# Feed-forwards: one 512-column and one 256-column matmul in place of three of 256, with the second half added by VectorE

## The chip, the cores and the metric

One core of a Trainium2 chip runs the whole program. The metric is the device time of one execution in microseconds (us).

## What is computed

Ten layers run one after the other on a sequence of 256 tokens of width 1024, in float32: an attention layer, feed-forward, convolution, feed-forward, neighbourhood attention, feed-forward, retention, feed-forward, convolution, feed-forward. Each is x + layer(norm(x)). The feed-forward (five of them) is

```python
h = _rmsnorm(x, norm_ffn_pre[l])
u = _dwconv(h @ w_up[l], conv_w[l], conv_b[l])
g, v = u[..., :D_FF], u[..., D_FF:]
y = (jax.nn.gelu(g, approximate=True) * v) @ w_down[l]
```

with D_FF = 2816 and a depthwise convolution of three taps along the tokens. The four later ones are of the same form.

## The kernel before

Tokens lie along the free axis (S = 256 columns) for the up products, and features on the 128 partitions. Every float32 factor is split in two parts, high (rounded to the format of the fast matmul) and low (the rest), and a product is three matmuls: high x high, low weight x high activation, high weight x low activation (`product`, lines 1971 to 1973; for the down products lines 2069 to 2071, with the activations as the stationary operand and 512 weight columns streamed). A matmul is always preceded by the load of its stationary operand.

All weights come as a stream of chunks of 128 x 2048 through a ring of three slots. SyncE loads chunk c into `raw` once the low part of chunk c - 3 is made; ScalarE makes the high part (`split_hi`, line 668; in the feed-forward loop `loop_split`, line 889) once TensorE is through with chunk c - 3; VectorE then makes the low part (`split_lo`, line 1154, and `loop_split`, line 1474); TensorE waits for that low part (`lo_done`) before it uses the chunk. Instructions of one engine run in the order in which they are written.

A feed-forward (`ffn`, on TensorE line 2156, ScalarE line 865, VectorE line 1424) has 22 tiles of 128 features. An up chunk holds the weights of one tile for both halves g and v: 2 x 8 steps of three 256-column matmuls, 48 in all. A down chunk serves two tiles: 24 matmuls of 512 columns into four banks. TensorE's order of chunks is up 0, 1, 2, 3, down 0, then up 4, 5, down 1 and so on to up 20, 21, down 9, and down 10. Chunk numbers in the text are those of this order; chunk 3 is the fourth up chunk and chunk 4 the first down chunk.

What happens to a tile behind its up chunk: VectorE scales both halves by the tokens' reciprocal roots (`up_norm`, line 1433); ScalarE makes the centre tap and bias (`centre`, line 877, two instructions); VectorE adds the outer taps (`taps`, line 1447, four instructions); ScalarE the gelu of half g (line 882); VectorE the product of the halves (`gated_value`, line 1456), its high part by a copy (`parts`, line 1466) and its low part (line 1468). The down chunk waits for that low part (`ulo_done`). The row of roots reaches every partition by a matmul in the second up chunk (`root_row`, line 1967), is copied by ScalarE (line 800), and VectorE's `up_norm(0)` waits for it.

The order on VectorE in a pair of tiles i is: parts(2i-2), low split of the second up chunk of the pair, low split of the down chunk, up_norm(2i), gated_value(2i-1), parts(2i-1), taps(2i), up_norm(2i+1), low split of the next pair's first up chunk, gated_value(2i), taps(2i+1).

In the neighbourhood attention (`attention`, lines 813 and 1346) ScalarE makes the high parts of the output projection's chunks 13 and 14 in four halves (`half_hi_of`, line 677) between the exponentials of the heads, and GpSimd their low parts in four pieces of 512 each (`low_parts`, line 587).

## Time and profile before

| | |
|---|---|
| time, median of 3 runs | 1617.42 us (1616.62 to 1617.46) |
| the profiled execution | 1617.76 us, span 1616.0 us |
| TensorE busy | 1594.0 us, 99% |
| VectorE busy | 1212.8 us, 75% |
| ScalarE busy | 897.1 us, 56% |
| GpSimd busy | 97.7 us, 6% |
| weights and other data read | 282.43 MB |

The time and the span are of the same execution; the 1.8 us between them lie outside the first and the last instruction. Busy times are of instructions; matmuls are pipelined and overlap in the record, so a mean duration of one is longer than what it holds TensorE up. The granted clock is a share of TensorE's full speed of 2.4 GHz.

### The profile page before, as it was taken

To read this page: it belongs to the slowest core of one execution; us is meant where nothing else is said; L and a number is where in the kernel's file an instruction comes from. 1 tells how busy PE (TensorE), PEld (TensorE's weight loads), DVE (VectorE), ACT (ScalarE), POOL (GpSimd) and SP (SyncE) were. 2 spreads that over 40 slices of the span, in tenths; PEclk is the share of its full clock that TensorE was granted. 3 is DMA by queue.
4 is the path that set the end of the run, shared out by engine and by line. 5 is a ranking of instruction groups with operands and counts; after the bars stand their busy time and mean duration, and the time that the engine had idled before them with its cause. 6 is when DMAs were issued, how large, how long until landed. Compare 5 with 4: busy or idle time off the path is not lost.

```text
span 1616.0 us, 28651 instructions
## 1 busy us (share of the span) xinstructions
PE 1594.0 (99%) x10570; PEld 1443.0 (89%) x10570; DVE 1212.8 (75%) x1828; ACT 897.1 (56%) x1190; POOL 97.7 (6%) x102
## 2 busy tenths in 40 slices
PE   9999999999999999989999999999999999999999
PEld 9888999978899999869999998878999987899998
DVE  6757887778787877856877886456787887878787
ACT  6576554565655546665544554544645456664553
POOL 0031000000000001330000042000100000000000
PEclk9999999999999999999999999999999999999999
DMA  9435545443654453443555455534554544345453
GB/s 344 147 115 178 199 182 204 160 169 118 241 187 178 182 208 133 171 142 131 184 190 198 180 185 183 203 109 157 175 214 169 184 179 183 133 155 204 185 182 130
DMA packets 43394, 285.48 MB, mean 177 GB/s; under 512 B 5280, under 2 KB 5408, under 8 KB 10688
## 3 DMA queue, kind: packets, MB, share of 16 engines
q1 hardware_dynamic: 40592, 274.96, 46.6%
q0 software_dynamic: 2736, 9.60, 1.8%
q8 instruction: 46, 0.75, 0.2%
q14 instruction: 20, 0.16, 0.0%
HBM read 282.43 MB, written 1.05 MB: 175 GB/s over the span
## 4 chain that ended last, share of the span: by engine, by line
PE 90%; DVE 5%; ACT 2%; issue 2%; DMA 1%; SPq 0%; POOL 0%; DVEq 0%; ACTq 0%
PE bank L1971 16%; PE bank L1973 16%; PE bank L1972 16%; PE bank L2069 8%; PE bank L2070 8%; PE bank L2071 8%; PE bank L2019 4%; PE bank L2020 4%; PE bank L2021 4%; PE bank L1953 1%; PE bank L2468 1%; DVE w_lo L1154 1%; PE bank L2130 1%; DMA x<-x_in 1%; DVE w_lo L1474 0%
## 5 line engine op out<-in xcount | busy, mean ns | idle before, releaser
L1971 PE MATMUL bank<-h_hi,w_hi 128*128 128x256 f32 x2220 | 633.5, 285 | 4.0 <-issue 2.3
L1972 PE MATMUL bank<-h_hi,w_lo 128*128 128x256 f32 x2220 | 630.2, 284 | 0.0
L1973 PE MATMUL bank<-h_lo,w_hi 128*128 128x256 f32 x2220 | 630.2, 284 | 0.0
L1971 PEld LDWEIGHTS bank<-h_hi,w_hi 128*128 128x128 f32 x2220 | 425.7, 192 | 11.2 <-issue 6.9
L1972 PEld LDWEIGHTS bank<-h_hi,w_lo 128*128 128x128 f32 x2220 | 425.7, 192 | 3.0
L1973 PEld LDWEIGHTS bank<-h_lo,w_hi 128*128 128x128 f32 x2220 | 425.6, 192 | 0.8
L1474 DVE TENSOR_TENSOR w_lo<-raw,w_hi 128x2048 fp32r<-128x2048 f32 x145 | 327.5, 2284 | 3.9 <-ACT w_hi L889 3.9
L877 ACT ACTIVATE arena<-arena,par 128x256 f32<-128x256 f32 x220 | 120.3, 594 | 352.2 <-DVE arena L1433 348.9
L1154 DVE TENSOR_TENSOR w_lo<-raw,w_hi 128x2048 fp32r<-128x2048 f32 (+3 forms) x108 | 232.8, 2156 | 103.3 <-ACT w_hi L668 103.2
L889 ACT ACTIVATE w_hi<-raw 128x2048 fp32r<-128x2048 f32 x150 | 286.2, 1908 | 19.8 <-PE bank L2071 19.8
L2069 PE MATMUL bank<-w_hi,h_hi 128*128 128x512 f32 x632 | 248.2, 393 | 1.5 <-DVE h_lo L1468 1.5
L2070 PE MATMUL bank<-w_lo,h_hi 128*128 128x512 f32 x632 | 246.6, 390 | 0.0
L2071 PE MATMUL bank<-w_hi,h_lo 128*128 128x512 f32 x632 | 246.0, 389 | 0.0
L668 ACT ACTIVATE w_hi<-raw 128x2048 fp32r<-128x2048 f32 (+3 forms) x105 | 187.9, 1791 | 102.0 <-PE bank L2071 38.9
L1447 DVE SCALAR_TENSOR_TENSOR arena<-arena,par 128x255 f32<-128x255 f32 x440 | 183.2, 478 | 22.4 <-ACT arena L877 22.4
L1433 DVE TENSOR_TENSOR arena<-bank,rs_row 128x512 f32<-128x512 f32 x110 | 76.0, 690 | 117.3 <-PE bank L1973 110.4
L2069 PEld LDWEIGHTS bank<-w_hi,h_hi 128*128 128x128 f32 x632 | 118.9, 188 | 27.1 <-issue 3.7
L2071 PEld LDWEIGHTS bank<-w_hi,h_lo 128*128 128x128 f32 x632 | 118.7, 188 | 25.2
L2070 PEld LDWEIGHTS bank<-w_lo,h_hi 128*128 128x128 f32 x632 | 118.9, 188 | 22.5 <-issue 0.2
L2019 PE MATMUL bank<-w_hi,h_hi 128*128 128x512 f32 x308 | 120.8, 392 | 0.1
L2020 PE MATMUL bank<-w_lo,h_hi 128*128 128x512 f32 x308 | 119.9, 389 | 0.0
L2021 PE MATMUL bank<-w_hi,h_lo 128*128 128x512 f32 x308 | 119.9, 389 | 0.0
(229 smaller groups left out, 1323.6 us busy)
## 6 DMA issues: line engine op xcount, KB each, us to landing
raw<-wstream SPq DMA_DIRECT2D x252, 1024.0 KB, 4.8
raw<-wstream SPq DMA_DIRECT2D x8, 256.0 KB, 3.8
raw<-wstream SPq DMA_DIRECT2D x4, 512.0 KB, 7.5
arena<-dilated_bias POOLq DMA_DIRECT2D x8, 256.0 KB, 4.7
arena<-conv_rows POOLq DMA_DIRECT2D x2, 1024.0 KB, 4.9
arena<-window_bias POOLq DMA_DIRECT2D x4, 512.0 KB, 5.8
raw<-wstream SPq DMA_DIRECT2D x4, 384.0 KB, 3.4
cst<-consts SPq DMA_DIRECT2D x1, 1088.0 KB, 12.6
```

The source lines that it names most:

```text
L668: nc.scalar.activation(w_hi[:, c % RING, 0:w], raw[:, c % RING, 0:w], ACT.Copy).then_inc(hi_done, 1)
L889: nc.scalar.activation(w_hi[:, c % RING, :], raw[:, c % RING, :], ACT.Copy).then_inc(hi_done, 1)
L1154: nc.vector.tensor_tensor(w_lo[:, s, 0:w], raw[:, s, 0:w], w_hi[:, s, 0:w].bitcast(F32), ALU.subtract)\
L1474: nc.vector.tensor_tensor(w_lo[:, c % RING, :], raw[:, c % RING, :], w_hi[:, c % RING, :].bitcast(F32), ALU.subtract).then_inc(lo_done, 1)
L1971: nc.tensor.matmul(dst, w_parts[0], x_parts[0], start=start, stop=False, **kw)
L1972: nc.tensor.matmul(dst, w_parts[1], x_parts[0], start=False, stop=False, **kw)
L1973: return nc.tensor.matmul(dst, w_parts[0], x_parts[1], start=False, stop=stop, **kw)
L2019: nc.tensor.matmul(dst, a, w[0], start=not second and t == 0, stop=False, skip_group_check=True)
L2020: nc.tensor.matmul(dst, a, w[1], start=False, stop=False, skip_group_check=True)
L2069: nc.tensor.matmul(dst, hi, w[0], start=first and a == 0, stop=False, skip_group_check=True)
L2070: nc.tensor.matmul(dst, hi, w[1], start=False, stop=False, skip_group_check=True)
L2071: last = nc.tensor.matmul(dst, lo, w[0], start=False, stop=last_ and a == 1, skip_group_check=True)
```

## The change

The high and the low part of the activations move into one array, side by side (`h_both`), and the eight banks of the accumulator become one array, two neighbouring banks for each of the two tiles in flight (`up_banks`). An up step is one matmul of 512 columns (high weights over high and low activations, into the two halves of a bank) and one of 256 (low weights over high activations, into the first half). ScalarE then copies the second halves of both banks to SBUF (`low_sums`), VectorE adds the first halves (`up_sum`) and in a second instruction scales. The high part of the gated product moves from VectorE to ScalarE (`high_part`), and the orders on both engines change; an up chunk waits for the add of the tile two before it, from tile 2 on. Row sums of the feed-forwards go to another bank. In the neighbourhood attention GpSimd makes both parts of chunks 13 and 14 (`both_parts`). Elsewhere views follow the new layout, with the same counts and widths. The diff, cut to what the text speaks of:

```diff
-        h_hi = sb("h_hi", [P, 16, S], F32R)
-        h_lo = sb("h_lo", [P, 16, S], F32R)
+        h_both = sb("h_both", [P, 16, 2, S], F32R)
+        h_hi, h_lo = h_both[:, :, 0, :], h_both[:, :, 1, :]
...
-        bank = [ctx.enter_context(nc.psum_tensor(f"bank{i}", [P, 512], F32)) for i in range(8)]
+        psum = ctx.enter_context(nc.psum_tensor("bank", [P, 8, 512], F32))
+        bank = [psum[:, (i + 1) % 8, :] for i in range(8)]
...
+        def up_banks(a):
+            return psum[:, 2 * a:2 * a + 2, :]
+        def row_bank(name):
+            return bank[DOWN0] if name.startswith("ffn") else stat
...
+        up_l = region(2560, 2, 512)
...
+            def both_parts(c, piece):
+                pool.wait_ge(raw_full[c % RING], 16 * (c // RING + 1))
+                pool.wait_ge(chunk_used, c - RING + 1)
+                pool.wait_ge(hi_done, c)
+                pool.wait_ge(lo_done, c)
+                for at in range(0, widths[c], piece):
+                    part, end = slice(at, at + piece), at + piece == widths[c]
+                    nc.gpsimd.tensor_copy(w_hi[:, c % RING, part], raw[:, c % RING, part]).then_inc(hi_done if end else piece_hi, 1)
+                    k["piece"] += not end
+                    pool.wait_ge(*((hi_done, c + 1) if end else (piece_hi, k["piece"])))
+                    last = nc.gpsimd.tensor_tensor(w_lo[:, c % RING, part], raw[:, c % RING, part],
+                                                   w_hi[:, c % RING, part].bitcast(F32), ALU.subtract)
+                last.then_inc(lo_done, 1)
...
-                        low_parts(c0 + c, 512)
+                        both_parts(c0 + c, 512)
...
+                def low_sums(t, a, used):
+                    act.wait_ge(chunk_used, used)
+                    if not isinstance(t, int) or t >= 2:
+                        act.wait_ge(up_sum, t + (T0 - 1))
+                    nc.scalar.activation(halves(up_l[:, a, :]), up_banks(a)[:, :, S:2 * S], ACT.Copy).then_inc(up_low, 1)
+                def high_part(t, slot, used=None):
+                    act.wait_ge(prod_done, t + (T0 + 1))
+                    if used is not None:
+                        act.wait_ge(chunk_used, used)
+                    nc.scalar.activation(h_hi[:, slot, :], u32[:, slot % 2, :], ACT.Copy).then_inc(uhi_done, 1)
+                low_sums(0, 0, c0 + 1)
                 centre(0, 0)
+                low_sums(1, 1, c0 + 2)
                 split_hi(c0 + 3)
                 centre(1, 1)
                 gelu(0, 0)
                 gelu(1, 1)
                 with act.Fori(1, FT // 2) as i:
+                    high_part(i * 2 + (-2), 8, i * 3 + (c0 - 1))
                     loop_split(i, 0)
-                    for a in range(2):
-                        centre(i * 2 + a, a)
-                        loop_split(i, 1 + a)
-                        gelu(i * 2 + a, a)
+                    high_part(i * 2 + (-1), 9, i * 3 + (c0 - 1))
+                    low_sums(i * 2, 0, i * 3 + c0)
+                    centre(i * 2, 0)
+                    loop_split(i, 1)
+                    low_sums(i * 2 + 1, 1, i * 3 + (c0 + 1))
+                    gelu(i * 2, 0)
+                    centre(i * 2 + 1, 1)
+                    loop_split(i, 2)
+                    gelu(i * 2 + 1, 1)
+                high_part(FT - 2, 10)
+                high_part(FT - 1, 11)
...
-                    attention((0, 1, 2), None, {2: lambda: half_hi_of(c0 + 13, 0), 3: lambda: half_hi_of(c0 + 13, 1),
-                                                5: lambda: half_hi_of(c0 + 14, 0), 6: lambda: half_hi_of(c0 + 14, 1)},
+                    attention((0, 1, 2), None, {},
...
+                    act.wait_ge(hi_done, c0 + 15)
...
-                def up_norm(t, a, bank_, used):
-                    dve.wait_ge(chunk_used, used)
+                def up_norm(t, a):
+                    dve.wait_ge(up_low, t + (T0 + 1))
                     if not isinstance(t, int) or t >= 2:
                         dve.wait_ge(taps_done, t * 4 + (4 * T0 - 4))
-                    nc.vector.tensor_tensor(halves(up_n[:, a, :]), halves(bank[bank_][:, :]),
+                    nc.vector.tensor_tensor(halves(up_n[:, a, :]), up_banks(a)[:, :, 0:S], halves(up_l[:, a, :]), ALU.add)\
+                             .then_inc(up_sum, 1)
+                    dve.wait_ge(up_sum, t + (T0 + 1))
+                    nc.vector.tensor_tensor(halves(up_n[:, a, :]), halves(up_n[:, a, :]),
                                             rs_row[:, :].unsqueeze(1).broadcast_to([P, 2, S]), ALU.mult).then_inc(up_ready, 1)
...
-                def parts(t, a, d_used=None):
-                    dve.wait_ge(prod_done, t + (T0 + 1))
-                    slot = 8 + a
-                    if d_used is None:
-                        slot = 10 + a
-                    else:
-                        dve.wait_ge(chunk_used, d_used)
-                    nc.vector.tensor_copy(h_hi[:, slot, :], u32[:, a, :]).then_inc(uhi_done, 1)
+                def low_part(t, slot):
                     dve.wait_ge(uhi_done, t + (T0 + 1))
-                    nc.vector.tensor_tensor(h_lo[:, slot, :], u32[:, a, :], h_hi[:, slot, :].bitcast(F32), ALU.subtract)\
+                    nc.vector.tensor_tensor(h_lo[:, slot, :], u32[:, slot % 2, :], h_hi[:, slot, :].bitcast(F32), ALU.subtract)\
                              .then_inc(ulo_done, 1)
...
                 prenorm(gain, c0)
-                up_norm(0, 0, c0 % 3, c0 + 1)
-                up_norm(1, 1, (c0 + 1) % 3, c0 + 2)
+                up_norm(0, 0)
+                up_norm(1, 1)
                 taps(0, 0)
                 split_lo(c0 + 3)
                 taps(1, 1)
                 gated_value(0, 0)
                 def two_tiles(i):
 
-                    used = i * 3 + (c0 - 1)
-                    parts(i * 2 + (-2), 0, used)
                     if not isinstance(i, int):
                         loop_split(i, -1)
+                    gated_value(i * 2 + (-1), 1)
+                    low_part(i * 2 + (-2), 8)
+                    low_part(i * 2 + (-1), 9)
+                    up_norm(i * 2, 0)
                     loop_split(i, 0)
-                    up_norm(i * 2, 0, (c0 + 2) % 3, i * 3 + c0)
-                    gated_value(i * 2 + (-1), 1)
-                    parts(i * 2 + (-1), 1, used)
                     taps(i * 2, 0)
-                    up_norm(i * 2 + 1, 1, (c0 + 3) % 3, i * 3 + (c0 + 1))
+                    up_norm(i * 2 + 1, 1)
                     loop_split(i, 1)
                     gated_value(i * 2, 0)
                     taps(i * 2 + 1, 1)
@@ -1500,9 +1551,9 @@
                 two_tiles(1)
                 with dve.Fori(2, FT // 2) as i:
                     two_tiles(i)
-                parts(FT - 2, 0)
                 gated_value(FT - 1, 1)
-                parts(FT - 1, 1)
+                low_part(FT - 2, 10)
+                low_part(FT - 1, 11)
...
-                def up(t, c, slot_c, between=None):
+                def up(t, a, c, slot_c, wait_h=None, between=None):
 
                     pe.wait_ge(lo_done, c + 1)
-                    if not isinstance(t, int) or t >= 3:
-                        pe.wait_ge(up_ready, t + (T0 - 1))
-                    for m in range(2):
-                        for kt in range(8):
-                            last = product(bank[slot_c % 3][:, m * S:(m + 1) * S], weights(slot_c, (8 * m + kt) * P),
-                                           h_parts(kt), kt == 0, kt == 7)
-                            if between and (m, kt) == (1, 2):
-                                between()
+                    if not isinstance(t, int) or t >= 2:
+                        pe.wait_ge(up_sum, t + (T0 - 1))
+                    steps = [(m, kt) for m in range(2) for kt in range(8)]
+                    if wait_h is not None:
+                        steps = [(m, kt) for kt in range(8) for m in range(2)]
+                    for m, kt in steps:
+                        if wait_h is not None and m == 0:
+                            pe.wait_ge(hlo_done, wait_h + kt + 1)
+                        w, dst = weights(slot_c, (8 * m + kt) * P), up_banks(a)[:, m, :]
+                        nc.tensor.matmul(halves(dst), w[0], h_both[:, kt, :, :], start=kt == 0, stop=kt == 7, skip_group_check=True)
+                        last = nc.tensor.matmul(dst[:, 0:S], w[1], h_hi[:, kt, :], start=False, stop=kt == 7, skip_group_check=True)
+                        if between and (m, kt) == (1, 2):
+                            between()
                     last.then_inc(chunk_used, 1)
...
-                feature_chunk(c0, wait_h=k["hlo"])
-                up(1, c0 + 1, c0 + 1, root_row)
-                up(2, c0 + 2, c0 + 2)
-                up(3, c0 + 3, c0 + 3)
+                up(0, 0, c0, c0, wait_h=k["hlo"])
+                up(1, 1, c0 + 1, c0 + 1, between=lambda: root_row(bank[DOWN0]))
+                up(2, 0, c0 + 2, c0 + 2)
+                up(3, 1, c0 + 3, c0 + 3)
                 down(0, c0 + 4, c0 + 4, first=True)
                 with pe.Fori(2, FT // 2) as i:
                     for a in range(2):
-                        up(i * 2 + a, i * 3 + (c0 - 1 + a), c0 + 2 + a)
+                        up(i * 2 + a, a, i * 3 + (c0 - 1 + a), c0 + 2 + a)
                     down(i - 1, i * 3 + (c0 + 1), c0 + 4)
```

## Rows read from the trace of the kernel before

**Rows 1.** Page, part 1: busy time, share of the span and instructions of each engine
```profile
PE 1594.0 (99%) x10570; PEld 1443.0 (89%) x10570; DVE 1212.8 (75%) x1828; ACT 897.1 (56%) x1190; POOL 97.7 (6%) x102
```

**Rows 2.** Groups by shape, TensorE: busy us, mean ns of one, idle before
```profile
L1971 PE MATMUL bank<-h_hi,w_hi 128*128 128x256 f32 x2200 | 625.6, 284 | 4.0 <-issue 2.3 <-DVE w_lo L1154 0.6 <-DVE w_lo L1277 0.3
```

**Rows 3.** Timeline, TensorE, second feed-forward (start us, us, engine, line)
```profile
430.62 0.35 PE L1971 MATMUL bank<-h_hi,w_hi 128*128 128x256 f32 x1
...
440.40 0.60 PE L1967 MATMUL bank<-hn,cst 128*128 128x256 f32 x2
...
440.95 0.28 PE L1972 MATMUL bank<-h_hi,w_lo 128*128 128x256 f32 x1
...
454.02 0.28 PE L1973 MATMUL bank<-h_lo,w_hi 128*128 128x256 f32 x1
...
454.14 0.40 PE L2069 MATMUL bank<-w_hi,h_hi 128*128 128x512 f32 x1
...
459.38 0.39 PE L2071 MATMUL bank<-w_hi,h_lo 128*128 128x512 f32 x1
...
459.82 0.38 PE L1971 MATMUL bank<-h_hi,w_hi 128*128 128x256 f32 x1
```

**Rows 4.** Timeline, VectorE, head of the second feed-forward
```profile
441.45 0.69 DVE L1433 TENSOR_TENSOR arena<-bank,rs_row 128x512 f32<-128x512 f32 x1 [1.32 <-ACT rs_row L800]
...
443.43 1.66 DVE L1447 SCALAR_TENSOR_TENSOR arena<-arena,par 128x255 f32<-128x255 f32 x4
...
445.11 2.29 DVE L1154 TENSOR_TENSOR w_lo<-raw,w_hi 128x2048 fp32r<-128x2048 f32 x1
...
449.68 0.43 DVE L1468 TENSOR_TENSOR h_lo<-arena,h_hi 128x256 fp32r<-128x256 f32 x1
...
450.88 2.29 DVE L1474 TENSOR_TENSOR w_lo<-raw,w_hi 128x2048 fp32r<-128x2048 f32 x1 [0.77 <-ACT w_hi L889]
```

**Rows 5.** Timeline, ScalarE, the same head
```profile
441.03 0.39 ACT L800 ACTIVATE rs_row<-bank 128x256 f32<-128x256 f32 x1 [1.71 <-PE bank L1967]
...
442.18 1.09 ACT L877 ACTIVATE arena<-arena,par 128x256 f32<-128x256 f32 x2 [0.76 <-DVE arena L1433]
...
443.18 1.90 ACT L668 ACTIVATE w_hi<-raw 128x2048 fp32r<-128x2048 f32 x1
...
447.37 0.42 ACT L882 ACTIVATE arena<-arena 128x256 f32<-128x256 f32 x1
```

**Rows 6.** Groups by shape, ScalarE and VectorE: nearest shapes to the added work
```profile
L998 ACT ACTIVATE h_hi<-arena 128x256 fp32r<-128x256 f32 x16 | 6.4, 420 | 6.5 <-DVE arena L1651 6.5
...
L988 ACT ACTIVATE arena<-bank 128x512 f32<-128x512 f32 x12 | 6.3, 599 | 4.4 <-PE bank L2268 4.4
...
L1896 DVE TENSOR_TENSOR arena<-arena 128x512 f32<-128x512 f32 x8 | 5.4, 689 | 1.9 <-ACT arena L1113 1.9
```

**Rows 7.** Timelines, TensorE and VectorE, tail of the second feed-forward
```profile
607.26 0.40 PE L2069 MATMUL bank<-w_hi,h_hi 128*128 128x512 f32 x1
...
607.57 0.69 DVE L1433 TENSOR_TENSOR arena<-bank,rs_row 128x512 f32<-128x512 f32 x1 [1.82 <-PE bank L1973]
...
612.62 0.42 DVE L1468 TENSOR_TENSOR h_lo<-arena,h_hi 128x256 fp32r<-128x256 f32 x1
...
613.19 0.47 PE L2069 MATMUL bank<-w_hi,h_hi 128*128 128x512 f32 x1 [0.30 <-DVE h_lo L1468]
```

**Rows 8.** Neighbourhood attention: timelines, stretches with granted clock, GpSimd's group
```profile
698.95 1.04 ACT L677 ACTIVATE w_hi<-raw 128x1024 fp32r<-128x1024 f32 x1
...
706.87 0.64 PE L2382 MATMUL bank<-cst,arena 128*128 128x128 f32 x2 [0.98 <-ACT arena L827]
...
703.55:706.96 3.41, 2.05 (x37) 1.34 (x36) 2.49 (x10) 3.41 (x8) 3.29 (x3) 1.00 0.01 2
...
706.97:710.38 3.41, 3.41 (x32) 2.52 (x32) 1.39 (x4) 2.21 (x8) 3.40 (x3) 0.50 0.65 226
...
L587 POOL TENSOR_TENSOR w_lo<-raw,w_hi 128x512 fp32r<-128x512 f32 x20 | 24.8, 1272 | 10.7 <-ACT w_hi L677 10.5
```

47 lines of the change are left out of this document (25 added, 22 removed).

## Prediction, made before the changed kernel ran

> **What bounds the kernel now.** The page comes first: TensorE is busy for 99% of the span and VectorE for 75% [rows 1], so a change that shortens TensorE's stream shortens the kernel, as long as the engines that feed it stay ahead. Then the groups by shape: the product helper (lines 1971 to 1973) issues 2200 steps of three 256-column matmuls [rows 2]; 22 tiles x 16 steps x 5 feed-forwards = 1760 of them are the ones that change. The mean of 284 ns is no price, since matmuls overlap; the price is the distance from start to start. In the second feed-forward 110 of the 256-column matmuls start between 440.95 and 454.02: 13.07 us over 109 distances, 120 ns; 24 of the 512-column ones start from 454.14 to 459.38: 5.24 us over 23, 228 ns [rows 3]. A matmul thus costs about 12 to 13 ns beyond its columns (two of 256 take 240, one of 512 takes 228). Last come the timelines of VectorE and ScalarE at the head and the tail of that stage, which the other four repeat at the same distances. TensorE stands still in a feed-forward in two places only: about 0.2 us ahead of the first chunk after the first down chunk (459.38 to 459.82 is 0.44 where 0.23 is the pace), and 0.46 us ahead of the last down chunk (613.19), behind a low part that ended at 613.04 [rows 3, 7].
>
> **What the change removes.** Columns stay the same (512 + 256 for 3 x 256), one matmul and its weight load go from each step. A step takes 3 x 120 = 360 ns now and 228 + 120 = 348 then; with the rounding of the starts 12 to 13 ns less, and I take 12.5. That is 352 x 12.5 ns = 4.4 us a stage and 22.0 us in all, if nothing else moves. The trace shows no 512-column load pair followed by a 256-column one on one half of a bank; the bounds are 0 (the fixed cost comes back as a wait for the next load) and 13.3 ns a step. I take 12.5, because the change from one width to the other at 454.02 to 454.14 costs no more than its 120 ns [rows 3].
>
> The Trainium skill's page "TensorE: Matmul & The Clock Gate", section "Back-to-back issue gap", speaks against the change: a warm matmul costs its columns and only about 2.5 ns more. By that figure the saving would be, as an estimate, 1760 x 2.5 ns = 4.4 us instead of 22.0. The rows of this trace show 12 to 13 ns and decide.
>
> **What it adds, and where the engines stand.** Durations: the new copy of the second half out of PSUM by ScalarE goes by the nearest 512-column copy from a bank, 0.60; the high part of the product on ScalarE by a 256-column copy to that same tile, 0.42; the scaling from SBUF by an SBUF product of 512, 0.69 [rows 6]; the add by the present scaling, 0.69 [rows 4]. One engine starts its next instruction 0.08 to 0.1 before the last one's end, a dependent one some 0.04 after it. Busy time is no bound: for a pair of tiles VectorE now needs about 3 x 2.2 (splits) + 8 x 0.4 (taps) + 2 x 0.6 (scaling) + 2 x 1.0 (product and its parts) = 13.0 us [rows 4]; the change adds 1.4 of scaling and takes off 0.6 of copies, and the pair will last 2 x 5.56 + 5.45 = 16.6.
>
> The order is. At the head of a stage, in the clock of the second feed-forward:
> - The row of roots (440.40) comes 27 steps x 12.5 ns = 0.34 earlier, at 440.06; ScalarE's copy of it ends at 441.08 in place of 441.42 [rows 3, 5].
> - Tile 0: ScalarE's copy to 441.71, add to 442.44, scaling to 443.17, the two centre taps (0.60 and 0.59, 0.5 apart) to 444.30. The third up chunk now waits for the add, not only for a free bank: it starts at 442.58 where TensorE could at 454.14 - 2 x 5.76 - 32 x 0.0125 = 442.2.
> - Only now does ScalarE copy tile 1 (444.2 to 444.8), and behind it the split of chunk 3 (1.90 [rows 5]) runs to 446.6. Add and scaling of tile 1 end at 446.27; taps of tile 0 start 446.2, the low split of chunk 3 at 447.8 and ends 450.1. Before, that split started at 445.11 [rows 4]. The fourth up chunk starts at 450.2; TensorE was ready at 442.58 + 5.56 = 448.1: a stall of 2.1.
> - VectorE: taps of tile 1 to 451.6, product 0 (0.42, like the low part of the product [rows 4]) to 451.9, product 1 to 452.3. ScalarE: high part 0 to 452.4, split of chunk 4 to 454.2, high part 1 to 454.5, copy of tile 2 to 455.1. VectorE: low part 1 to 455.0, add and scaling of tile 2 to 456.5, and only behind that the low split of chunk 4, the first down chunk, 456.4 to 458.7. Before, it ran at 450.88 to 453.17, ahead of the scaling [rows 4].
> - The first down chunk therefore starts at 458.8 in place of 454.14: 4.7 later, though three to four faster up chunks lie ahead of it. TensorE is ready at 455.8, a stall of 3.0.
>
> From there on TensorE sets the pace. In a steady period the low split of the down chunk waits behind the scaling of the even tile: 0.31 (end of the stream to the reader, 607.26 to 607.57 [rows 7]) + 0.60 + 0.69 + 0.69 + 2.28 + 0.2 of steps between = 4.8, and the next up chunk covers 16 x 0.3475 = 5.56: 0.8 us to spare. The 18 up chunks left give back 18 x 16 x 12.5 ns = 3.6, and the old stall of 0.2 ahead of the fifth goes: -3.8.
>
> At the tail (chunk of tile 21 read from 607.57 on): copy to 608.17, add to 608.90, scaling to 609.63, low split of the last chunk to 611.83, product 20 to 612.17, third tap of tile 21 to 613.37, gelu (0.42 [rows 5]) to 613.8, product 21 to 614.3; ScalarE's high part 20 stands behind that gelu (to 614.2) and VectorE's low part 20 behind product 21 (to 614.6). The last down chunk starts at 614.75 in place of 613.19 [rows 7]: +1.55. The next stage starts behind the down sums and moves with them.
>
> Sum of one feed-forward: 4.7 - 3.8 + 1.55 = +2.4, with +-1.2 for the eight or so hand-offs in each chain; five of them: +12.
>
> **The neighbourhood layer.** Chunks 13 and 14 lose their high halves on ScalarE: four pieces of 1.04 us between the exponentials. TensorE waits for ScalarE right behind them, 0.98 at 706.87 and as long at one other [rows 8]. And behind this stretch its clock falls to 0.50, the 1.2 GHz level, for 706.97 to 710.38, after 3.41 us in which it was busy for 2.05 with small matmuls [rows 8]. Bounds: no gain, if VectorE's maxima come just as late; 4 x 0.95 + 3.41/2 = 5.5 if every piece and the clock's fall go. I take -2, the two long waits, and call the fall open. GpSimd takes on eight copies beside its eight differences of 1.27 [rows 8]: 8 x (1.27 + 0.5 to 1.27) = 14 to 20 us from about 699, where ScalarE's first piece stands now, thus done by 719. Chunk 14 is read two output chunks (2 x 5.45) behind the end of the attention, which still runs at 706.97 to 710.38 [rows 8]: not before 721. Hidden; if its pieces took twice as long, up to 18 us of it would show. The shared layout and the renumbered banks change no count and no width: nothing, hidden by nothing.
>
> **Sum.** Against the profiled execution (1617.76, span 1616.0, median 1617.42): span 1616.0 + 12 - 2 = 1626, and 1617.4 + 10 = 1627 for the time.
>
> **Rivals.**
> 1. *The covers hold, faster.* The head and tail chains hide, and TensorE runs through. It decides whether the low split of the first down chunk ends before 455.7 instead of 458.7, and the one of chunk 3 before 448. Price: 1617.4 - 22 - 1 (old stalls) - 2 = 1592. For: VectorE is idle 25% [rows 1]. Against: the order is written out, and each link has a row.
> 2. *The clock falls behind the new stalls.* TensorE would be idle 3.0 us, run on a first down chunk at 0.50, and lose up to 3.41/2 = 1.7 us in each stage [rows 8]: +4 to +8.5, so 1631 to 1636. For: the one fall of the trace came after 2.05 of 3.41 busy, and here it would be less. Against: no standstill of some 3 us in the middle of a dense stream is in the trace, so what it does there is open. The skill's same page, section "HAM oscillation — how this bites in real kernels", tells of kernels whose clock is halved after gaps between bursts; no run here shows it for a dense stream.
> 3. *Half the stalls.* The two head chains overlap better than worked (each 1 us shorter a stage, the tail hidden): 1617.4 + 5 x (2.4 - 2.5) - 2 = 1615, no change within the measurement.
> 4. *VectorE sets the steady pace.* From 0.8 us more in the chain above, each us costs 45 periods x 1: if the copy took 1.6, +4, at 1.8 +13 more: 1640. Against: the nearest copy takes 0.60 [rows 6].
>
> **Chances.** Worked case 0.55 (1627, 1621 to 1632); rival 1 0.13; rival 2 0.20; rival 3 0.08; rival 4 0.04. Range 1610 to 1636: leaves out rivals 1 and 4 and a little of the others. Faster by over 0.2% (3.2 us, about what a measurement of this kernel can tell): 0.16, within it 0.08, slower 0.76.
>
> **What would show it.** Starts of the steady up matmuls 348 ns a step apart; the fourth up chunk about 7.6 us after the third in place of 5.76; the first down chunk about 28 us after the first up matmul in place of 23.5 (454.14 - 430.62 [rows 3]); the low split of that chunk behind the scaling of tile 2; no stall in the nine periods behind; the last down chunk about 2 us late. Wrong would be: a step that stays at 360 (then +22 more), or a first down chunk that starts before 456.

## The result and the profile after

| | before | after |
|---|---|---|
| time, median of 4 runs each | 1617.02 us | 1642.58 us (1641.73 to 1643.99) |
| ratio, 95% interval | | 1.0162 (1.0150 to 1.0174) |
| profiled execution, span | 1617.76 us, 1616.0 us | 1641.98 us, 1640.2 us |
| two up chunks / one down chunk, steady | 11.51 / 5.47 us | 11.29 / 5.50 us |

The change makes the kernel 1.6% slower. The forecast was slower, but by 10 us and not by 25, and the time lies above its range of 1610 to 1636.

The page of after, part 1 (busy time of each engine), answers to [rows 1]; the lines under it are from its part 5 and answer to [rows 2]:

```profile
PE 1589.3 (97%) x8810; PEld 1351.3 (82%) x8810; DVE 1249.1 (76%) x1828; ACT 996.1 (61%) x1406; POOL 102.4 (6%) x110
...
L2228 PE MATMUL bank<-h_both,w_hi 128*128 128x512 f32 x1760 | 625.3, 399 | 9.0 <-DVE w_lo L1208 8.1
L2229 PE MATMUL bank<-h_both,w_lo 128*128 128x256 f32 x1760 | 493.7, 281 | 0.0
...
L2125 PE MATMUL bank<-w_hi,h_both 128*128 128x512 f32 x632 | 252.4, 399 | 23.5 <-DVE w_lo L1525 14.1
```

TensorE issues 1760 matmuls fewer, and is busy for 97% of the span in place of 99%. The last column holds what is new: it stands still for 8.1 us ahead of up chunks and for 14.1 us ahead of down chunks behind VectorE's low splits; most of the other 9.4 of the 23.5 us lie ahead of the last down chunks. The mean durations of 399 and 281 ns are as little a price as the 284 ns of [rows 2].

Where in the program: the trace cut at the first transposes of each layer gives the length of each stage (us, worked out from their starts). The head of a feed-forward is what lies ahead of its first down chunk, the tail what lies behind its last up chunk; a clock fall is a stretch in which the granted clock is 0.50, the 1.2 GHz level.

| stage | before | after | difference | clock falls in it (after) |
|---|---|---|---|---|
| feed-forward 1 | 194.49 | 198.83 | +4.34 | none |
| feed-forward 2 | 190.25 | 196.40 | +6.15 | at 462.8 |
| neighbourhood attention | 124.37 | 120.77 | -3.60 | none (before: at 707) |
| feed-forward 3 | 190.30 | 196.04 | +5.74 | at 780.2 |
| feed-forward 4 | 190.27 | 194.50 | +4.23 | none |
| feed-forward 5 | 193.69 | 201.14 | +7.45 | at 1469.7 and 1630.1 |
| the four others | 532.59 | 532.51 | -0.08 | none |

The feed-forwards are 27.9 us longer and the neighbourhood attention 3.6 shorter: +24.2, the difference of the spans. The first and the fourth, whose clock held, give the price of the change without falls, 4.3 us; the other three carry 1.85, 1.45 and 3.15 us more, 6.4 in all. Of these 6.4, 0.4 is no clock fall but a longer stall at the tail of the second. The neighbourhood attention's 3.6 hold a clock fall of the profiled execution of before, of which more below.

Timeline of TensorE, head and tail of the second feed-forward of after. Its first up matmul starts at 434.87, so its clock is 4.25 us ahead of that of [rows 3]:

```profile
452.53 0.28 PE L2229 MATMUL bank<-h_both,w_lo 128*128 128x256 f32 x1
...
454.41 0.50 PE L2228 MATMUL bank<-h_both,w_hi 128*128 128x512 f32 x1 [1.60 <-DVE w_lo L1208]
...
459.95 0.28 PE L2229 MATMUL bank<-h_both,w_lo 128*128 128x256 f32 x1
...
463.11 0.79 PE L2125 MATMUL bank<-w_hi,h_both 128*128 128x512 f32 x1 [2.88 <-DVE w_lo L1525]
463.70 0.63 PE L2126 MATMUL bank<-w_lo,h_both 128*128 128x512 f32 x1
464.12 0.63 PE L2127 MATMUL bank<-w_hi,h_both 128*128 128x512 f32 x1
...
623.56 0.47 PE L2125 MATMUL bank<-w_hi,h_both 128*128 128x512 f32 x1 [2.17 <-DVE h_both L1519]
```

The columns are those of [rows 3]; the bracket gives the idle time before and what ended it. The first down chunk starts 463.11 - 434.87 = 28.24 us behind the first up matmul (23.52 before), the fourth up chunk behind a stall of 1.60, the last down chunk behind one of 2.17. At 463 the matmuls of 512 columns last 0.63 and stand 0.42 apart in place of 0.39 and 0.23: the clock has fallen.

Timeline of VectorE, the same head:

```profile
446.09 0.69 DVE L1488 TENSOR_TENSOR arena<-bank,arena 128x512 f32<-128x512 f32 x1 [1.70 <-ACT arena L927]
...
449.15 0.69 DVE L1488 TENSOR_TENSOR arena<-bank,arena 128x512 f32<-128x512 f32 x1 [1.65 <-ACT arena L927]
...
452.06 2.29 DVE L1208 TENSOR_TENSOR w_lo<-raw,w_hi 128x2048 fp32r<-128x2048 f32 x1
...
459.43 0.69 DVE L1488 TENSOR_TENSOR arena<-bank,arena 128x512 f32<-128x512 f32 x1
460.16 0.69 DVE L1491 TENSOR_TENSOR arena<-arena,rs_row 128x512 f32<-128x512 f32 x1
460.76 2.29 DVE L1525 TENSOR_TENSOR w_lo<-raw,w_hi 128x2048 fp32r<-128x2048 f32 x1
```

Less the offset of 4.25, the low split of chunk 3 starts at 447.81 (forecast 447.8; 445.11 before [rows 4]) and that of the first down chunk at 456.51 (forecast 456.4; 450.88 before), right behind the add and the scaling of tile 2. VectorE waits for ScalarE's copies (line 927), twice for 1.7 us. The durations of the new operations, groups by shape:

```profile
L927 ACT ACTIVATE arena<-bank 128x512 f32<-128x512 f32 x110 | 65.3, 594 | 101.6 <-PE bank L2229 101.6
...
L1491 DVE TENSOR_TENSOR arena<-arena,rs_row 128x512 f32<-128x512 f32 x110 | 76.2, 692 | 3.7
...
L614 POOL CAST w_hi<-raw 128x512 fp32r<-128x512 f32 x8 | 4.9, 612 | 0.2 <-POOL w_lo L617 0.2
```

594 and 692 ns stand against the 0.60 and 0.69 taken from [rows 6].

What the forecast got wrong sits between head and tail. Timeline of TensorE in the first feed-forward, first before, then after (its last line is the last down chunk of the stage):

```profile
165.63 0.40 PE L2069 MATMUL bank<-w_hi,h_hi 128*128 128x512 f32 x1
...
188.39 0.28 PE L1971 MATMUL bank<-h_hi,w_hi 128*128 128x256 f32 x1
...
199.90 0.40 PE L2069 MATMUL bank<-w_hi,h_hi 128*128 128x512 f32 x1
...
205.37 0.28 PE L1971 MATMUL bank<-h_hi,w_hi 128*128 128x256 f32 x1
```

```profile
170.27 0.50 PE L2125 MATMUL bank<-w_hi,h_both 128*128 128x512 f32 x1 [2.88 <-DVE w_lo L1525]
...
192.62 0.39 PE L2228 MATMUL bank<-h_both,w_hi 128*128 128x512 f32 x1
...
203.91 0.40 PE L2125 MATMUL bank<-w_hi,h_both 128*128 128x512 f32 x1
...
209.42 0.39 PE L2228 MATMUL bank<-h_both,w_hi 128*128 128x512 f32 x1
...
328.93 0.47 PE L2125 MATMUL bank<-w_hi,h_both 128*128 128x512 f32 x1 [1.80 <-DVE h_both L1519]
```

Two up chunks (32 steps) take 199.90 - 188.39 = 11.51 us before, 360 ns a step, and 203.91 - 192.62 = 11.29 after, 353 ns. The forecast was 347.5. The down chunk behind them went from 5.47 to 5.50. A pair of tiles thus takes 16.79 us in place of 16.98, where 16.57 was expected, and no stall is to be seen in it. The first down chunk here stands behind the same 2.88 us of stall as in the second feed-forward, and its clock held.

### The profile page after: what moved, and what is told of

Read it like the earlier page. It is cut to its first block, busy times and chain, and to the rows that moved or that the text cites. A ratio compares the mean times of both kernels' runs of the same rounds, so it can differ in the third digit from the quotient of the medians.

```text
span 1640.2 us, 25659 instructions
## 1 busy us (share of the span) xinstructions
PE 1589.3 (97%) x8810; PEld 1351.3 (82%) x8810; DVE 1249.1 (76%) x1828; ACT 996.1 (61%) x1406; POOL 102.4 (6%) x110
## 4 chain that ended last, share of the span: by engine, by line
PE 85%; DVE 8%; ACT 3%; issue 2%; DMA 1%; SPq 0%; POOL 0%; DVEq 0%; ACTq 0%
PE bank L2228 23%; PE bank L2229 11%; PE bank L2125 8%; PE bank L2127 8%; PE bank L2126 8%; PE bank L2075 4%; PE bank L2076 4%; PE bank L2077 4%; PE bank L2022 3%; PE bank L2023 2%; PE bank L2024 2%; DVE w_lo L1208 2%; DVE arena L1505 1%; DVE w_lo L1525 1%; PE bank L2004 1%
## 5 line engine op out<-in xcount | busy, mean ns | idle before, releaser
L2228 PE MATMUL bank<-h_both,w_hi 128*128 128x512 f32 x1760 | 625.3, 399 | 9.0 <-DVE w_lo L1208 8.1
L2229 PE MATMUL bank<-h_both,w_lo 128*128 128x256 f32 x1760 | 493.7, 281 | 0.0
L2228 PEld LDWEIGHTS bank<-h_both,w_hi 128*128 128x128 f32 x1760 | 330.6, 188 | 93.4 <-DVE w_lo L1208 9.7
L2229 PEld LDWEIGHTS bank<-h_both,w_lo 128*128 128x128 f32 x1760 | 332.2, 189 | 1.9
L2125 PE MATMUL bank<-w_hi,h_both 128*128 128x512 f32 x632 | 252.4, 399 | 23.5 <-DVE w_lo L1525 14.1
L2127 PE MATMUL bank<-w_hi,h_both 128*128 128x512 f32 x632 | 249.3, 394 | 0.0
L2126 PE MATMUL bank<-w_lo,h_both 128*128 128x512 f32 x632 | 248.6, 393 | 0.0
L2125 PEld LDWEIGHTS bank<-w_hi,h_both 128*128 128x128 f32 x632 | 120.1, 190 | 53.1 <-DVE w_lo L1525 15.7
L2127 PEld LDWEIGHTS bank<-w_hi,h_both 128*128 128x128 f32 x632 | 119.9, 190 | 27.0
L2126 PEld LDWEIGHTS bank<-w_lo,h_both 128*128 128x128 f32 x632 | 120.5, 191 | 23.9 <-issue 0.2
L2022 PE MATMUL bank<-h_both,w_hi 128*128 128x256 f32 (+1 forms) x460 | 133.7, 291 | 3.9 <-issue 2.3
L2023 PE MATMUL bank<-h_both,w_lo 128*128 128x256 f32 (+1 forms) x460 | 132.3, 288 | 0.0
L2024 PE MATMUL bank<-h_both,w_hi 128*128 128x256 f32 (+1 forms) x460 | 132.2, 287 | 0.0
L2075 PE MATMUL bank<-w_hi,h_both 128*128 128x512 f32 x308 | 120.8, 392 | 0.1
```

The costliest lines, as they stand in the source:

```text
L2022: nc.tensor.matmul(dst, w_parts[0], x_parts[0], start=start, stop=False, **kw)
L2075: nc.tensor.matmul(dst, a, w[0], start=not second and t == 0, stop=False, skip_group_check=True)
L2125: nc.tensor.matmul(dst, hi, w[0], start=first and a == 0, stop=False, skip_group_check=True)
L2126: nc.tensor.matmul(dst, hi, w[1], start=False, stop=False, skip_group_check=True)
L2127: last = nc.tensor.matmul(dst, lo, w[0], start=False, stop=last_ and a == 1, skip_group_check=True)
L2228: nc.tensor.matmul(halves(dst), w[0], h_both[:, kt, :, :], start=kt == 0, stop=kt == 7, skip_group_check=True)
```

## The experiments

### Is it the order on the feeding engines that costs?

One kernel rewrites the order alone (the texts below call it run order). At the head the first two pairs of tiles and at the tail the last pair are written out, and each split stands ahead of the work on the tile that TensorE doesn't wait for yet (copy, add, scaling, centre tap); in the loop the splits move forward too. `up_norm` is cut in two. ScalarE's and VectorE's heads, from the diff against the changed kernel:

```diff
                 low_sums(0, 0, c0 + 1)
+                split_hi(c0 + 3)
+                low_sums(1, 1, c0 + 2)
                 centre(0, 0)
-                low_sums(1, 1, c0 + 2)
-                split_hi(c0 + 3)
+                split_hi(c0 + 4)
+                gelu(0, 0)
                 centre(1, 1)
-                gelu(0, 0)
+                split_hi(c0 + 5)
...
-                up_norm(0, 0)
-                up_norm(1, 1)
+                up_add(0, 0)
+                up_scale(0, 0)
+                split_lo(c0 + 3)
+                up_add(1, 1)
                 taps(0, 0)
-                split_lo(c0 + 3)
+                up_scale(1, 1)
+                split_lo(c0 + 4)
+                gated_value(0, 0)
                 taps(1, 1)
-                gated_value(0, 0)
...
```

> The changed kernel with all its instructions, but another order of them on ScalarE and VectorE at the head (first two pairs) and the tail (last pair) of a feed-forward, and the splits ahead of the scaling in the loop. By the chain of durations no stall of TensorE is left but some 0.1 us at the third up chunk: a stage is 184.9 instead of 191.9 from the first up matmul to the end of the last down chunk, and without stalls the clock does not fall in the feed-forwards: 1642 - 35 - about 6 = 1601 us, faster than the kernel before by 16. If the stalls come from something that the order does not reach (the reads of the banks, the queue, a busier VectorE), most of them stay and the time stays above 1630.

Measured: 1599.76 us against 1616.23, ratio 0.9901 (0.9885 to 0.9918). The same matmuls as in the changed kernel now make a kernel that is 1.0% faster than before, not 1.6% slower (2.3 of these 16.5 us come from the neighbourhood attention, see its section). Timeline of TensorE, its first feed-forward:

```profile
141.68 0.48 PE L2274 MATMUL bank<-h_both,w_hi 128*128 128x512 f32 x1
...
164.80 0.28 PE L2275 MATMUL bank<-h_both,w_lo 128*128 128x256 f32 x1
164.92 0.39 PE L2171 MATMUL bank<-w_hi,h_both 128*128 128x512 f32 x1
```

The first down chunk starts 23.24 us behind the first up matmul (28.24 after, 23.53 before), with no bracket: no stall. The five stages are 2.7 to 3.1 us shorter than before (the second 187.48 in place of 190.25), and no clock fall is left in them. Its steady chunks are those of after, 11.29 and 5.50.

Two kernels take one end of that order each, with the loop's old order. The first:

> The changed kernel with the new order of run order at the head of a feed-forward alone (the first two pairs of tiles), loop and tail as the change has them. If head and tail are two separate prices, the head's 5.0 us of stalls a stage go (187.0 instead of 191.9 from the first up matmul to the end), the 2.0 ahead of the last down chunk stay, and so do the clock's falls only where a stall of about 3 us was the cause: 1642 - 25 - 5 = about 1611. If the stall at the tail is a late effect of the head (VectorE never catches up), it goes too: 1601.

Measured: 1609.11 against 1616.44, ratio 0.9955 (0.9940 to 0.9970); stage 2 takes 189.42, no falls, and the one stall left is the 1.7 us ahead of the last down chunk. The other:

> The changed kernel with the new order of run order at the tail of a feed-forward alone (the last pair of tiles); head and loop as the change has them. The 2.0 us ahead of the last down chunk go, the head's 5.0 stay: 189.8 a stage instead of 191.9, 10 us in all, and falls of the clock stay behind the head's stalls: about 1632. If the tail's stall hangs on the head, it stays: above 1638.

Measured: 1633.90 against 1616.44, ratio 1.0099 (1.0084 to 1.0115). Stage 2 takes 195.26; the stalls of 1.6 and 2.8 us are there, the tail's is gone, and the clock falls behind the head's stall in all five, and once more in the neighbourhood attention. The two kernels are 24.8 us apart, of which the falls are a part.

One kernel undoes only the place of the first down chunk's low split:

```diff
-                    up_norm(i * 2, 0)
-                    loop_split(i, 0)
+                    if isinstance(i, int):
+                        loop_split(i, 0)
+                        up_norm(i * 2, 0)
+                    else:
+                        up_norm(i * 2, 0)
+                        loop_split(i, 0)
```

> The changed kernel with one move on VectorE: in the first pair of tiles alone, the low split of the first down chunk stands ahead of the scaling of tile 2, as it did before the change. If that place alone makes the 3 us stall, it goes and five stages save 15 us (about 1628). By the chain worked out link by link, VectorE has too much work queued there: the stall ahead of the first down chunk shrinks from about 3.0 to 1.5, and 2.9 appear ahead of the next up chunk, because its low split now waits behind the late scaling of tile 3; a stage gets 1.5 us longer: about 1650 us.

Measured: 1648.63, ratio 1.0201 (1.0184 to 1.0218). Timeline of TensorE, second feed-forward:

```profile
462.31 0.28 PE L2233 MATMUL bank<-h_both,w_lo 128*128 128x256 f32 x1
...
463.89 0.50 PE L2129 MATMUL bank<-w_hi,h_both 128*128 128x512 f32 x1 [1.30 <-DVE w_lo L1525]
...
472.57 0.49 PE L2232 MATMUL bank<-h_both,w_hi 128*128 128x512 f32 x1 [2.96 <-DVE w_lo L1525]
```

The stall of 2.88 becomes 1.30, and the fifth up chunk gets one of 2.96: the split ahead holds up the add of tile 2, and all of the queue behind it. In the fourth feed-forward, where the clock held in both kernels, the stage takes 195.95 us in place of 194.50, the 1.5 that was worked out. Moving one link of a chain that is late as a whole moves the stall, and makes it longer.

### What does a step cost?

> The changed kernel with the merged matmul undone: three matmuls of 256 columns a step, the third into the second half of the bank; the copy, the add, the orders and the layout stay. If the stalls at the head and the tail of a feed-forward come from the order of ScalarE's and VectorE's work, they stay (about 1.8 ahead of the fourth up chunk, 2.9 ahead of the first down chunk, 2.0 ahead of the last), each step costs 360 ns instead of 353, and a stage is 2.3 us longer than in the changed kernel where the clock holds: 5 x 2.3 = 11, about 1653 us. The clock should still fall in some stages, since the stalls are the same. The rival, that the 512-column matmul itself brings the stalls, the slower neighbours and the clock's falls, expects the time to drop towards 1617.

This kernel has three matmuls of 256 columns in the changed kernel's frame (the third goes to the second half with its own start; what it computes is not the full product, and only its times are used). Measured: 1651.16, ratio 1.0210 (1.0193 to 1.0228); two up chunks take 11.52 us, as before. Compared in the first feed-forward, where neither has a fall, the changed kernel saves 200.70 - 198.83 = 1.87 us. Of these, 1.74 lie between the first down chunk and the last but one (152.94 against 151.20 us, worked out from the starts), which is 6.0 ns for each of the 288 steps there, not 12.5. The stalls stay with the old widths, 1.5 and 2.7 us at the head and 1.8 to 2.2 at the tail, and the clock falls in four of the five feed-forwards.

Where the other half went, four kernels ask, all with the new order. The first lets the low weights' matmul write the other half of the bank:

```diff
-                        last = nc.tensor.matmul(dst[:, 0:S], w[1], h_hi[:, kt, :], start=False, stop=kt == 7, skip_group_check=True)
+                        last = nc.tensor.matmul(dst[:, S:2 * S], w[1], h_hi[:, kt, :], start=False, stop=kt == 7, skip_group_check=True)
```

> The kernel of run order, but the low weights' matmul of 256 columns adds to the second half of the bank instead of the first; the sum of the halves is the same. If the 6 ns of a step come from the distance between two writes to the same columns of a bank (512 columns back for the narrow, 256 for the next wide one), they change here, since the narrow one now writes what the wide one has just written: either down to 347 or further up. If they come from the alternation of widths or from the wide matmul itself, nothing changes: 353 a step and 1600 us.

Measured: 1600.24, 0.9896 (0.9880 to 0.9913), 11.29 us for two up chunks. Which half the second matmul writes makes no difference.

> The kernel of run order, but the low weights also stream both activation parts: two matmuls of 512 columns a step (it adds the low-by-low term, which the other kernels leave out). If the alternation of widths costs the 6 ns, all starts stand 227 apart, 454 a step, and 1760 x 101 ns = 178 us come on top: 1778. If a 512-column matmul over the two parts is slow by itself, 236 and 472 a step: 1810 us.

Measured: 1773.57, one execution. Here the second matmul has 512 columns as well, which adds a product of the low parts. Timeline of TensorE:

```profile
499.66 0.39 PE L2275 MATMUL bank<-h_both,w_lo 128*128 128x512 f32 x1
499.88 0.39 PE L2274 MATMUL bank<-h_both,w_hi 128*128 128x512 f32 x1
500.11 0.39 PE L2275 MATMUL bank<-h_both,w_lo 128*128 128x512 f32 x1
500.34 0.39 PE L2274 MATMUL bank<-h_both,w_hi 128*128 128x512 f32 x1
```

0.68 us over three distances is 227 ns; two up chunks take 14.51, 64 x 226.7. A wide matmul over both halves, on the same operands and the same bank, costs what any of 512 costs. With 119.9 for a narrow one (11.51 us over 96) a step should take 346.6. Alternated, it takes 352.8: 6.2 ns more than its two parts.

Next, the kernel with eight wide (512 columns), then eight narrow ones (256) for each half tile:

> The kernel of run order, with the matmuls of a half tile grouped by width: first the eight of 512 columns, then the eight of 256 (the very first up chunk of a stage keeps the old order). Question: a step of one 512 and one 256 takes 353 ns (236 + 117) where 227 + 120 = 347 was worked out from the rows. If the alternation of widths costs the 6 ns, starts stand 227 and 120 apart here and 105 of 110 up chunks give back 16 x 6 ns each: 10 us, about 1590. If a 512-column matmul over the two activation parts is slower by itself, the wide ones stay 236 apart; then the narrow ones tell whether they get 117 or 120: 1600 to 1605. If the length of the matmul ahead of a weight load matters, the first narrow one alone moves.

Measured: 1595.49 against 1617.20, ratio 0.9865 (0.9848 to 0.9881), above the 1590 that was expected. The steps give back 4.5 ns each and not 6; the third up chunk now waits 0.67 us for the add of tile 0 in the first and the second feed-forward, whose waits were read; and the profiled execution has a clock fall in the neighbourhood attention. Timeline of TensorE, first feed-forward; the line at 188.53 follows a down chunk:

```profile
188.53 1.98 PE L2282 MATMUL bank<-h_both,w_hi 128*128 128x512 f32 x8
190.34 1.11 PE L2287 MATMUL bank<-h_both,w_lo 128*128 128x256 f32 x8
191.30 2.00 PE L2282 MATMUL bank<-h_both,w_hi 128*128 128x512 f32 x8
193.14 0.28 PE L2287 MATMUL bank<-h_both,w_lo 128*128 128x256 f32 x1
```

Last, a kernel in which widths change once a step instead of twice:

```diff
-                        nc.tensor.matmul(halves(dst), w[0], h_both[:, kt, :, :], start=kt == 0, stop=kt == 7, skip_group_check=True)
-                        last = nc.tensor.matmul(dst[:, 0:S], w[1], h_hi[:, kt, :], start=False, stop=kt == 7, skip_group_check=True)
+                        wide = lambda: nc.tensor.matmul(halves(dst), w[0], h_both[:, kt, :, :], start=kt == 0, stop=kt == 7, skip_group_check=True)
+                        narrow = lambda: nc.tensor.matmul(dst[:, 0:S], w[1], h_hi[:, kt, :], start=False, stop=kt == 7, skip_group_check=True)
+                        for part in ((wide, narrow) if kt % 2 == 0 else (narrow, wide)):
+                            last = part()
```

> The kernel of run order with the order inside a step turned in every second step: wide, narrow, narrow, wide, wide, narrow and so on, so that half of the changes of width are gone. If each change of width costs, half of the 6 ns a step goes: 350 a step, 1595 us. If the wide matmul itself is slow, nothing moves: 353 and 1600.

Measured: 1590.30, one execution, below what was expected (three quarters of the 6 ns come back, not half); and the same kernel again, for an interval:

> The kernel of run o_pairs again, timed against the kernel before: both theories of the step's price left it to one look. 1590 us, faster than the kernel before by 1.65% (ratio 0.983 to 0.985); if the one look was a lucky one, it lies at the 1600 of run order.

Measured: 1591.04 against 1616.44, ratio 0.9841 (0.9828 to 0.9855). This version beats both kernels: 1.6% under the one before, 3% under the changed one. Timeline of TensorE, first feed-forward, a steady pair of tiles:

```profile
187.13 0.39 PE L2274 MATMUL bank<-h_both,w_hi 128*128 128x512 f32 x1
187.36 0.40 PE L2275 MATMUL bank<-h_both,w_lo 128*128 128x256 f32 x2
187.59 0.63 PE L2274 MATMUL bank<-h_both,w_hi 128*128 128x512 f32 x2
...
198.27 0.39 PE L2171 MATMUL bank<-w_hi,h_both 128*128 128x512 f32 x1
...
203.72 0.39 PE L2274 MATMUL bank<-h_both,w_hi 128*128 128x512 f32 x1
```

| order of a step's matmuls | two up chunks | a step | down chunk | a pair of tiles |
|---|---|---|---|---|
| three of 256 (before) | 11.51 | 360 | 5.47 | 16.98 |
| wide, narrow, wide, narrow | 11.29 | 353 | 5.50 | 16.79 |
| eight wide, eight narrow | 11.15 | 348 | 5.46 | 16.61 |
| wide, narrow, narrow, wide | 11.14 | 348 | 5.44 | 16.59 |

The forecast's 348 ns and 16.6 us are what the last two orders reach. What costs the 4.6 ns that the alternating one takes more is not settled: it is not the half that is written, nor the wide matmul itself. One change of width per step (the last row) costs as little as one per eight matmuls (the row above), so a fixed price for each change doesn't fit either.

The rows do show where the price sits. In the grouped kernel eight wide matmuls behind the wide ones of a down chunk take 190.34 - 188.53 = 1.81 us, and eight behind narrow ones 193.14 - 191.30 = 1.84. So a change from narrow to wide is paid behind the first wide matmul, in the distances that follow it. The trace of before has it too, where the first down chunk follows narrow ones at 454.14 [rows 3]:

```profile
455.53 0.39 PE L2069 MATMUL bank<-w_hi,h_hi 128*128 128x512 f32 x1
```

The six distances from 454.14 to 455.53 are 232 ns each, the 17 from there to 459.38 are 226.5. In the alternating stream of after, the mean distance is 236 ns behind a wide matmul and 117 behind a narrow one, 233 and 115 in the paired order (worked out from the starts in the first feed-forward).

### Does the stall bring the clock down, or the new matmuls?

The kernel before, with nothing changed but two idle differences of 2048 columns on VectorE (into scratch, each waited for) ahead of the first down chunk's low split:

```diff
+                    if isinstance(i, int):
+                        dve.wait_ge(hi_done, c0 + 5)
+                        s4 = (c0 + 4) % RING
+                        for _ in range(2):
+                            nc.vector.tensor_tensor(xs[:, :, :], halves(raw[:, s4, :]), halves(w_hi[:, s4, :].bitcast(F32)),
+                                                    ALU.subtract).then_inc(late, 1)
...
```

> The kernel before, with nothing of the change, but two idle differences of 2048 columns on VectorE ahead of the low split of the first down chunk in each feed-forward. They make TensorE wait about 3.7 us ahead of that chunk and 1 us ahead of the next up chunk, in the midst of a dense stream of 256- and 512-column matmuls. VectorE's 2 x 2.33 us show in full: 5 x 4.6 = 23, about 1640 us, if the clock holds. If a stall of 3 us or more is what makes the clock fall, its falls to 0.50 appear in some of the five stages, right behind the stall, each for 3.4 us and 1.7 us of time: 1642 to 1648. If the falls in the changed kernel came from its matmuls or banks, none appears in a feed-forward here.

Measured: 1645.36 against 1616.55, ratio 1.0177 (1.0148 to 1.0207). Stretches of its second feed-forward (length, then busy time and count of TensorE, its loads, VectorE, ScalarE and GpSimd, then TensorE's granted clock, the DMA share and GB/s), and under them those of after:

```profile
462.60:466.00 3.40, 0.45 (x4) 0.25 (x3) 3.37 (x2) 0.00 (x0) 0.00 (x0) 1.00 0.00 0
466.00:472.80 6.80, 6.18 (x15) 4.83 (x16) 6.41 (x11) 4.79 (x7) 0.00 (x0) 0.50 0.42 154
472.90:479.70 6.80, 6.80 (x50) 6.38 (x49) 6.47 (x10) 3.54 (x3) 0.00 (x0) 1.00 0.49 159
```

```profile
459.40:462.81 3.41, 0.83 (x6) 0.46 (x4) 3.35 (x3) 1.72 (x3) 0.00 (x0) 0.99 0.01 2
462.81:466.22 3.41, 3.11 (x7) 2.48 (x8) 3.38 (x8) 1.98 (x4) 0.00 (x0) 0.51 0.46 159
466.30:469.70 3.40, 3.40 (x17) 2.80 (x16) 3.40 (x6) 2.81 (x3) 0.00 (x0) 1.00 0.44 147
```

With the old matmuls and a stall of 3.57 us the granted clock falls to 0.50, the 1.2 GHz level, in all five feed-forwards, around the late start of the first down chunk (and once in a convolution). So the stall is enough, without the new matmuls. In after, the stretch with the stall of 2.88, in which TensorE is busy for 0.83 of 3.41 us, is followed by one at 0.51, with 7 matmuls where the next has 17. The falls of all runs, read from the granted clock and the stalls of the profiled executions:

| kernel | stall of TensorE | feed-forwards with a fall at it |
|---|---|---|
| before, with the idle differences | 3.57 us | five of five |
| after, first down chunk | 2.8 to 2.9 | three of five |
| three matmuls of 256 in its frame, first down chunk | 2.7 | four of five |
| new order at the tail alone, first down chunk | 2.7 to 2.8 | five of five |
| down split moved, fifth up chunk | 2.9 to 3.3 | three of five |
| after, last down chunk | 1.8 to 2.2 | one of five |
| the frame of 256, down split moved and new order at the head alone, last down chunk | 1.7 to 2.2 | none of fifteen |

A fall starts between 0.8 us before and 1.4 us behind the end of its stall. The one at a short stall is the second of after's fifth feed-forward, behind 1.81 us:

```profile
1626.70:1630.11 3.41, 1.60 (x8) 1.04 (x7) 3.17 (x9) 2.02 (x4) 0.00 (x0) 1.00 0.00 0
```

The cost of a fall: from the first down chunk to the down chunk of tiles 18 and 19 the second feed-forward of after gained 0.50 us on before where the first gained 1.93, so the fall took 1.4; the same working gives 1.6 in the third and in the fifth, and 1.6 for the one at the end. The Trainium skill's page "TensorE: Matmul & The Clock Gate", section "HAM oscillation — how this bites in real kernels", describes this for bursts that wait for data; here it comes from one stall in an otherwise dense stream. Why nearly equal stalls brought the clock down in three stages of after and not in the first and the fourth stays open. How many falls there are is not fixed by the kernel either: its four executions have mean granted clocks of 0.994 to 0.996, and the longest is 2.3 us above the shortest.

### The neighbourhood attention by itself

> The kernel before with only the edit of the neighbourhood attention: GpSimd makes both parts of chunks 13 and 14, ScalarE none. If the 3.6 us by which that layer is shorter in the changed kernel come from this edit, they show here alone: 1613.5 us, and no fall of the clock at 707 us. If they come from the new layout or from the layer before, nothing moves (1617).

Measured: 1613.91 against 1616.23, ratio 0.9985 (0.9975 to 0.9995). Only `both_parts` and the missing high halves are in it, on the kernel before. The stage takes 120.73 us in place of 124.37. Its stretches, same columns:

```profile
703.40:706.80 3.40, 3.04 (x48) 2.12 (x44) 2.15 (x8) 3.08 (x11) 3.16 (x4) 1.00 0.02 5
706.80:710.20 3.40, 2.72 (x43) 1.91 (x42) 3.11 (x11) 2.51 (x8) 3.24 (x4) 1.00 0.65 236
```

TensorE is busy for 3.04 of 3.40 us where it was for 2.05 of 3.41 [rows 8], and the clock holds in these two stretches. That the edit keeps the clock up is not shown, though. Other kernels with this edit have the fall here all the same (eight wide matmuls in a row, new order at the tail alone, and the paired order in one of its two profiled executions): their stage takes 121.93 to 121.97. And the kernel before with the idle differences, which lacks the edit, has no fall here: 123.12. So the edit is worth 2.4 us, with the fall (124.37 - 121.95) and without it (123.12 - 120.73), and the fall costs 1.2 by itself. The medians agree, 1616.23 - 1613.91 = 2.3. Of the 13 executions of before that were timed with this run nine have a mean granted clock of 1.000 and take 1615.7 to 1616.4 us, and four a lower one and 1617.2 to 1617.8.

## Why the forecast was wrong, step by step

- **The head, +4.7: right.** 28.24 - 23.53 = 4.71 in the first feed-forward. The links read above came within about 0.1 us: split of chunk 3 at 447.81 for 447.8, fourth up chunk at 450.16 for 450.2, split of the first down chunk at 456.51 for 456.4, its start at 458.86 for 458.8. The stalls by the brackets were 1.60 and 2.88 for 2.1 and 3.0; the forecast counted from start to start, and so counted they were 454.41 - 446.93 - 5.64 = 1.84 and 463.11 - 454.41 - 5.64 = 3.06 (446.93 is the start of the third up chunk, 5.64 half of 11.29).
- **The tail, +1.55: right.** From the start of the last but one down chunk to that of the last, 328.93 - 321.47 = 7.46 us after and 5.93 before [rows 7]: +1.53. In the second feed-forward it was 1.90; what the 0.4 more comes from is open.
- **Between them, -3.8: wrong, -1.9.** This is the term that failed, "I take 12.5, because the change from one width to the other costs no more than its 120 ns": it priced an alternated step at 347.5 ns, and it took 352.8. From 171.31 to 318.76 before and 175.83 to 321.47 after, 147.45 and 145.64 us for 18 up chunks and 8 down chunks: 1.81 us over 288 steps, 6.3 ns for each; with 0.12 from the old gap ahead of the fifth up chunk, 1.9. The bound below (0) had held the case, but I priced the middle by one change of width per chunk, and the change makes two per step. The reading of that one change was wrong as well: the distance from 454.02 to 454.14 lies ahead of the first wide matmul, and what the change costs stands behind it (232 ns a distance up to 455.53). That is 1.9 us in each stage, 9.5 in all. The Trainium skill's page "TensorE: Matmul & The Clock Gate", section "Back-to-back issue gap", gives a fixed cost of about 2.5 ns for an isolated matmul. The chunks show 13.3 (119.9 less the 106.7 of 256 columns at 2.4 GHz, 226.7 less 213.3), so the row was rightly taken over the page, and neither said what alternation does.
- **The clock: the case with the chance of 0.20 came, in part.** Rival 2 had the mechanism and the price (up to 1.7 a fall; 1.4 to 1.6 measured) and was wrong in adding it to a sum that was itself too low. There were four falls in three stages, one of them behind the tail's stall, where the forecast had none. Together with small differences at heads and tails (+0.4 at the second tail) they are the +6.4 that the stages show.
- **The neighbourhood attention, -2: right in kind, -3.6 in size.** The edit gave 2.4; the other 1.2 is a fall that the profiled execution of before happened to have, and no work of the change. GpSimd's copies took 0.61 us, inside the 0.5 to 1.27.
- Together: +10 forecast for the span, +9.5 for the steps, +6.4 for the falls and the second tail, -1.6 for the neighbourhood attention: 24.3, and 24.2 is measured.
- **Rival 1 (the covers hold, 1592)** was false for this kernel, but true of the matmuls: with the order mended, and mixed widths paired, 1591.0 is what they give. **Rival 3** fell with the head's 4.7. **Rival 4** fell too: no stall in the nine steady periods, and ScalarE's copy took 594 ns. Its price was added up wrongly: with 0.8 us to spare a copy of 1.6 would cost 0.2 x 45 = 9 us and one of 1.8 18, not 4 and 13.

The likeliest case and rival 2 should have been one case with a range for the step of 348 to 360, not two cases at 348; with the step at its bound of 360 the text itself had "+22 more", above the range that was given.

## What to carry to other kernels

Work taken off the engine that bounds the kernel pays only as far as the engines that feed it keep their order of urgency: replay their queues link by link at the head and the tail of each loop, where no surplus has been built up, and move whole chains, not one link. Price a new mix of matmul widths from chunk lengths of that mix; where it doesn't exist yet, the fixed cost seen in equal widths is a bound for the saving and not the saving. A stall of about 3 us in a dense stream can cost 1.4 to 1.6 us more by the clock, so taking it away can pay for itself and half as much again. Before a difference of a microsecond is put down to an edit, look whether a clock fall stands in one of the two profiles.

## What the runs showed of the hardware

Matmuls of 512 and of 256 columns in turn take 352.8 ns a pair, 6.2 more than 226.7 + 119.9; in the order wide, narrow, narrow, wide they take 348.2. The price of a change from narrow to wide shows behind the first wide matmul (232 ns a distance for six, then 226.5), not ahead of it. The granted clock fell to its 1.2 GHz level at a single stall of 2.7 to 3.6 us in a stream that was dense before and after, in three to five of five equal places, for 3.4 or 6.8 us, and at stalls of 1.7 to 2.2 us in one of twenty. A fall of 3.4 us took 1.2 to 1.6 us. The same kernel had the fall in the neighbourhood attention in one execution and not in another.
